# VectorE takes half of the picks of three items, gathered by pick column, into x_out

## The reference, cut to what matters

```
t = rms_norm(x, g_ffn)
q = t @ w_q                                  # 8 heads, two halves of 64
s = q . sub_keys; top 16 of each half; sums of pairs; top 16 of 256 -> ids, gates = softmax
act = gelu(einsum('td,thkd->thk', t, expert_u[ids]))
x  += einsum('thk,thkd->td', gates * act, expert_v[ids])
```

## Time and profile before

| | |
|---|---|
| median of 3 runs | 3340.63 us |
| profiled execution, its span | 3345.7 us, 23941 instructions |
| PE, PEld | 2192.0 us (66%), 765.3 us (23%) |
| DVE | 2166.7 us (65%) |
| ACT | 306.1 us (9%) |
| POOL | 2069.9 us (62%) |
| DMA | 1201.37 MB, mean 359 GB/s |

### The profile page before, as it was taken

The page is one execution under the profiler, slowest core; times in us unless marked ns, Lnnn a source line. Parts: engine busy times, 40 slices in busy tenths (PEclk is TensorE's granted clock), DMA queues, the critical chain, the costliest instruction groups (busy, mean ns, idle before and its releaser), DMA issues.

```text
span 3345.7 us, 23941 instructions
## 1 busy us (share of the span) xinstructions
PE 2192.0 (66%) x7260; PEld 765.3 (23%) x7260; DVE 2166.7 (65%) x5654; ACT 306.1 (9%) x657; POOL 2069.9 (62%) x2196
## 2 busy tenths in 40 slices
PE   8366776557644774688955376657895627564498
PEld 6112322112212121123312122212331212110122
DVE  4868488758777767635387967864618797636500
ACT  3100111101000001010101000000010010000000
POOL 1565665666666665566665656666666665666665
PEclk9698888778877987789977687878997868776699
DMA  6799998999999999999998999999999999999998
GB/s 248 286 365 332 368 363 329 378 379 343 373 368 339 367 374 409 410 400 365 364 362 324 385 337 359 368 365 383 360 356 343 349 365 332 384 373 377 380 375 326
DMA packets 331693, 1201.37 MB, mean 359 GB/s; under 512 B 40999, under 2 KB 41385, under 8 KB 329516
## 3 DMA queue, kind: packets, MB, share of 16 engines
q0 software_dynamic: 313344, 1140.99, 89.8%
q1 hardware_dynamic: 16988, 49.42, 3.9%
q10 hardware_dynamic: 1232, 9.44, 0.7%
HBM read 1188.82 MB, written 10.87 MB: 359 GB/s over the span
## 4 chain that ended last, share of the span: by engine, by line
DVE 26%; POOL 25%; issue 15%; another core or an unknown queue 15%; PE 13%; DMA 5%; ACT 1%; DVEq 0%; ACTq 0%; POOLq 0%
POOL rows L691 25%; DVE rows L1732 11%; PE acc L1208 7%; DVE psB L1405 4%; DMA rows<-in_expert_v,idsT 2%; DMA rows<-in_expert_u,ids 2%; PE psB L1143 1%; DVE work L1493 1%; DVE work L1486 1%; DVE work L1483 1%; PE psA L1056 1%; DVE work L1527 1%; DVE work L1533 1%; DVE work L1539 1%
## 5 line engine op out<-in xcount | busy, mean ns | idle before, releaser
L1208 PE MATMUL acc<-rows,strip 128*32 128x512 f32 x4352 | 1394.8, 658 | 462.9 <-DMA rows<-in_expert_v,idsT 305.0
L1732 DVE CUSTOM_DVE_ANT_0 rows<-rows,psH 128x1024 f32<-128x1024 f32 x1088 | 1288.3, 1218 | 336.2 <-DMA rows<-in_expert_u,ids 227.6
L691 POOL DMA_INDIRECT rows<-in_expert_v,idsT x1088 | 1030.6, 947 | 619.6 <-issue 273.0
L691 POOL DMA_INDIRECT rows<-in_expert_u,ids x1088 | 1024.1, 941 | 604.0 <-issue 326.0
L1208 PEld LDWEIGHTS acc<-rows,strip 128*32 128x32 f32 x4352 | 338.7, 116 | 1431.8 <-issue 955.0
L1405 DVE SCALAR_TENSOR_TENSOR psB<-zbuf,chan,psB 128x128 f32<-128x128 f32 (+1 forms) x827 | 202.8, 328 | 21.3 <-DVE psB L1405 16.6
L999 PE MATMUL psA<-w_out_sb,hT 128*128 128x512 f32 x288 | 153.8, 680 | 47.2 <-issue 35.1
L1039 PE MATMUL psB<-w_in_sb,hT 128*128 128x512 f32 x288 | 143.8, 649 | 56.9 <-DVE hT L1386 31.1
L1143 PE MATMUL psB<-w_q_sb,hT 128*128 128x512 f32 x288 | 142.0, 643 | 57.9 <-issue 37.5
L1739 DVE TENSOR_TENSOR x_out<-acc,x_out 128x1024 f32<-128x1024 f32 x10 | 12.2, 1222 | 248.9 <-PE acc L1208 176.6
L1056 PE MATMUL psA<-w_in_sb,hT 128*128 128x512 f32 x288 | 141.5, 646 | 1.7 <-DVEq L1573 1.7
(11 more groups left out here) (227 smaller groups left out, 1403.9 us busy)
## 6 DMA issues: line engine op xcount, KB each, us to landing
rows<-in_expert_u,ids POOLq DMA_INDIRECT x1088
rows<-in_expert_v,idsT POOLq DMA_INDIRECT x1088
w_in_sb<-in_w_in SPq DMA_DIRECT2D x4, 2176.0 KB, 30.7
w_out_sb<-in_w_out SPq DMA_DIRECT2D x2, 4096.0 KB, 18.6
w_q_sb<-in_w_q SPq DMA_DIRECT2D x2, 4096.0 KB
x_out<-x_mid SPq DMA_DIRECT2D x10, 512.0 KB
w_in_sb<-in_w_in ACTq DMA_DIRECT2D x2, 2176.0 KB, 22.8
x_mid<-x_mix SPq DMA_DIRECT2D x8, 512.0 KB
```

The source lines that it names most:

```text
L691: nc.gpsimd.indirect_dma_start(out=rows[:, j, :], out_offset=None, in_=table[:, :], in_offset=bass.IndirectOffsetOnAxis(ap=index, axis=0))\
L1208: last = nc.tensor.matmul(acc[LS * a:LS * (a + 1), half:half + 512], strip[:, first:first + LS], rows[:, at % RING, half:half + 512], star ...
L1732: nc.vector.tensor_tensor_reduce(rows[:, j, :], rows[:, j, :], psH[:, :], 1.0, 0.0, ALU.mult, ALU.add, dots[:, r:r + 1]).then_inc(s_free[j ...
```

## The change

The 128 picks of items 3, 6 and 9 are parted (SHARED = {3: 2, 6: 2, 9: 2}). Picks 0 to 63 are summed by TensorE as before, but in the quartered order, with 64 v gathers in place of 128. Picks 64 to 127 become a third kind of gather, "w": partition t gets the expert_v row of token t's r-th pick (index ids[:, r]), and VectorE adds coef[:, r] times this row to x_out. The w gathers of items 3 and 6 stand in ticks 12 to 26 of loops 4 and 7, where there is no v gather left; those of item 9 stand between its last 16 v gathers in loop 10. The number of gathers, 2176, and their bytes stay.

```diff
+SHARED = {3: 2, 6: 2, 9: 2}
...
+V_SHARED = [2] * 8 + [6, 7, 7, 6] + [0] * 15 + [2.5] * 8 + [2, 0, 4, 4, 2, 2, 2]
+W_WEIGHT = [0] * 12 + [2] + [4] * 12 + [7, 7] + [0] * 15
...
-V_OWN = {..., 4: V_ALONE, ..., 7: V_ALONE, 8: V_SHORT}
+V_OWN = {..., 4: V_SHARED, ..., 7: V_SHARED, 8: V_SHORT}
...
-          3: ..., 4: [(0, 36, 3, 0, 128), (37, 42, 4, 0, 14)],
+          3: ..., 4: [(0, 36, 3, 0, 64), (37, 42, 4, 0, 14)],
...
-          6: ..., 7: [(0, 36, 6, 0, 128), (37, 42, 7, 0, 14)],
+          6: ..., 7: [(0, 36, 6, 0, 64), (37, 42, 7, 0, 14)],
...
-          10: [(0, 42, 9, 48, 128)]}
+          10: [(0, 42, 9, 48, 64)]}
+
+W_PLAN = {4: (12, 27, 3, W_WEIGHT), 7: (12, 27, 6, W_WEIGHT), 10: (0, 42, 9, [1] * 42)}
...
-          ("both", 9, (10, 20), (11, 0))]
+          ("both", 9, (10, 0), (11, 0))]
...
+    def by_fours(v):
+        return v < QUARTERED or v in SHARED
+
+    def sums(v):
+        return SPICK * SHARED[v] if v in SHARED else width(v)
...
+    def w_at(n, tick):
+        if n not in W_PLAN:
+            return []
+        t0, t1, v, weight = W_PLAN[n]
+        return [("w", v, r) for r in share(weight, t0, t1, sums(v), picks(v), tick)]
...
+                elif kind == "w":
+                    table, index = ev, ids[:, i:i + 1]
...
+            def clear(v, g, k):
+                if g < 2 and v and by_fours(v) != by_fours(v - 1):
+                    for q in range(0, 1) if by_fours(v) else range(1, COPIES):
+                        step(nc.scalar.copy(laid_off(q)[:, k % 2 * GROUP:(k % 2 + 1) * GROUP], strip[:, 0:GROUP]))
+                    settle()
...
-                    if m < QUARTERED:
+                    if by_fours(m):
                         for part in range(QUARTERS):
                             last = turn_quarter(psA[:, LS * part:LS * (part + 1)], idf[m], part)
...
-                turn_tile(n, psH, coef).then_inc(s_cturn, 1)
+                if n in SHARED:
+                    for part in range(QUARTERS):
+                        last = turn_quarter(psH[:, LS * part:LS * (part + 1)], coef, part)
+                else:
+                    last = turn_tile(n, psH, coef)
+                last.then_inc(s_cturn, 1)
...
+            def add_picks(v, r):
+                j = AT["w", v, r] % RING
+                if r == sums(v):
+                    dve.wait_ge(s_coef, weighed(v))
+                    dve.wait_ge(s_xo, moved(1 + next(i for i, (what, u, _, _) in enumerate(X_PLAN) if u == v and what != "norm")))
+                else:
+                    done(dve, ("w", v, r - 1))
+                landed(dve, ("w", v, r))
+                nc.vector.scalar_tensor_tensor(out=x_out[:, :], in0=rows[:, j, :], scalar=coef[:, r:r + 1],
+                                               in1=x_out[:, :], op0=ALU.mult, op1=ALU.add).then_inc(s_free[j], 1)
...
             def take_sums(i, v):
                 n = spread(v)
                 done(dve, last_v(v))
+                if v in SHARED:
+                    done(dve, ("w", v, picks(v) - 1))
...
-                    picked = u_at(n, tick)
+                    picked = u_at(n, tick) + w_at(n, tick)
```

More of the change, by code:

```diff
@@ L53 @@
 V_LIGHT = [1] * 8 + [4] * 4 + [0.5] * 13 + V_LATE
[L54 removed]
+V_OWN = {0: V_QUARTERS[0], 1: V_QUARTERS[1], 2: V_CONV, 3: V_LIGHT, 4: V_SHARED, 5: V_SHORT, 6: V_LIGHT, 7: V_SHARED, 8: V_SHORT}
 U_END = [27, 27, 26, 26, 8, 26, 26, 8, 26, 26]
@@ L184, in build @@
     FETCHES = opening() + [key for n in range(ITEMS + 1) for tick in range(0 if n else 6, TICKS)
-                           for key in v_at(n, tick) + u_at(n, tick)]
+                           for key in v_at(n, tick) + u_at(n, tick) + w_at(n, tick)]
     AT = {key: i for i, key in enumerate(FETCHES)}
@@ L198, in last_v @@
     def last_v(v):
-        return "v", v, width(v) - 1
+        return "v", v, sums(v) - 1
     def place(v, i):
-        return i % 4, i % LS // 4 if v < QUARTERED else i // 4
+        return i % 4, i % LS // 4 if by_fours(v) else i // 4
     def index_column(v, i):
         a, b = place(v, i)
-        return SPICK * (i // LS) + 8 * a + b if v < QUARTERED else per_band(v) * a + b
+        return SPICK * (i // LS) + 8 * a + b if by_fours(v) else per_band(v) * a + b
     def per_band(v):
@@ L216, in spread @@
         return P if is_sample(v) else width(v)
-    GROUPS = [(v, g) for v in range(ITEMS) for g in range(width(v) // GROUP)]
+    GROUPS = [(v, g) for v in range(ITEMS) for g in range(sums(v) // GROUP)]
     def groups_at(n, tick):
@@ L836, in lay_out_quarter @@
                     done(act, ("v", u, GROUP * (ahead + 1) - 1))
+                clear(v, g, k)
                 for q in range(COPIES):
@@ L839, in lay_out_quarter @@
                     dst = laid_off(q)[r, k % 2 * GROUP:(k % 2 + 1) * GROUP].rearrange("p (b a) -> p b a", a=4)
-                    src = coefT[r, v, LS * part:LS * (part + 1)].rearrange("p (a b) -> p b a", a=4)
+                    src = coefT[r, v % 2, LS * part:LS * (part + 1)].rearrange("p (a b) -> p b a", a=4)
                     step(nc.scalar.copy(dst, src[:, 2 * g4:2 * g4 + 2, :]))
@@ L850, in lay_out @@
                     done(act, ("v", u, GROUP * (before + 1) - 1))
-                if v == QUARTERED and g < 2:
-                    for q in range(1, COPIES):
-                        step(nc.scalar.copy(laid_off(q)[:, k % 2 * GROUP:(k % 2 + 1) * GROUP], strip[:, 0:GROUP]))
-                    settle()
+                clear(v, g, k)
                 dst, src = laid[:, k % 2 * GROUP:(k % 2 + 1) * GROUP], coefT[:, v % 2, 0:width(v)]
@@ L934, in _ @@
                     for v, g in groups_at(n, tick):
-                        if v < QUARTERED:
+                        if by_fours(v):
                             lay_out_quarter(v, g)
@@ L1204, in add_tokens @@
                     a, b = place(v, i)
-                    first = (k % 2 * GROUP + i % GROUP + 1) * LS - 1 - (QUARTERS * b if v < QUARTERED else b)
-                    start, stop = i < 4, i + 4 >= width(v)
+                    first = (k % 2 * GROUP + i % GROUP + 1) * LS - 1 - (QUARTERS * b if by_fours(v) else b)
+                    start, stop = i < 4, i + 4 >= sums(v)
                     for half in (0, 512):
@@ L1733, in take_row, with take @@
                                                ALU.mult, ALU.add, dots[:, r:r + 1]).then_inc(s_free[j], 1)
+            def add_picks(v, r):
[8 more added lines that the diff above has]
+                                               in1=x_out[:, :], op0=ALU.mult, op1=ALU.add).then_inc(s_free[j], 1)
+            def take(key):
+                kind, m, r = key
+                if kind == "u":
+                    take_row(m, r)
+                else:
+                    add_picks(m, r)
             def take_sums(i, v):
@@ L1783, in _ @@
                                 if picked:
-                                    take_row(n, picked.pop(0)[2])
+                                    take(picked.pop(0))
                             weigh(n, part)
@@ L1792, in _ @@
                             if picked:
-                                take_row(n, picked.pop(0)[2])
-                    for _, _, r in picked:
-                        take_row(n, r)
+                                take(picked.pop(0))
+                    for key in picked:
+                        take(key)
 _INS = ['x_prompt', 'x_sample', 'state_pool', 'state_dwconv', 'state_shortconv', 'g_mix', 'w_in', 'w_pool',
```

## The result

The kernel after takes 3375.57 us (median of 4 runs, 3369.77 to 3385.29) against 3339.24 us for the kernel before on the same chip. The ratio is 1.0125 with a 95% interval of 1.0107 to 1.0142, or 36 us slower by the medians. Forecast was no change. The profiled execution has a span of 3383.4 us, 37.7 more than the span of before.

The account below looks back on a forecast made before the run. The prediction took the kernel as bound by its stream of 2176 gathers, held in places by engine chains. Terms +1.0 - 0.2 - 2.0 - 0.6 + 2.7 = +0.9 us on 3340.6 gave 3341.5 us, range 3320 to 3366.

Parts of the forecast that it names:

- Ticks 0 to 11: First part of loops 4 and 7, paced by the DMA: 74 gathers instead of 81, 110.1 us and 106.5 us.
- The w step: VectorE's addition in ticks 12 to 26: 1.28 us each, 1.32 apart in step with GpSimd, no cost from the shared port.
- TensorE is no hindrance: Ticks 12 to 26: norms, query and scores fit between w steps (45.0 us busy of 110.9); the 28.97 us wait goes.
- From the first w gather to the routing: Loops 4 and 7: 5.8 us landing, 84.5 w steps, 4.7 other VectorE work, 2 waits make 97.0; 97.4 us taken.
- Routing with what follows: Last part of loops 4 and 7, from the routing's start to the gather it releases: 65.6 and 68.8 us.
- about 74 us: Beside loop 4's routing: the time in which the DMA has 62 us of work, from 43 gathers.
- 12 for the one at the end: GpSimd's wait for TensorE near the end of loops 4 and 7 grows from 5 to about 12 us.
- Loop 10: Last 80 gathers, 64 moved to VectorE: 1.41 us each for 1.44, -2.0 us; landing to sum -0.6 more.
- The 410 GB/s of the trace: Stream rate seen late in loop 9, 1.28 us a gather; it kept a faster pace possible.
- The turns: 16 small matmuls turning expert numbers between routing and the next item's sums, 0.9 us three times: +2.7 us.
- the slow one: Rival: w steps in ticks 12 to 26 over 1.32 us apart, from port-delayed gathers or mixer waits; 3368.5 us, chance 0.22.
- point of decision: The slow rival decides from about 1.32 us a w step on, where loop 4's sum breaks even.

Follow-up runs that it names:

- after_again: The kernel after, unchanged, run again on one of the slower chips: ratio 1.0128 to the kernel before.
- half_steps: The kernel after with w steps on columns 0 to 511 only, upper half of the w picks' sum left out: 1.0113 to the kernel before.
- tensor_kept_going: The kernel after with 90 added TensorE matmuls that change no sum in ticks 12 to 26 of loops 4 and 7: 1.0196 to the kernel before.
- order_of_item_9: The kernel before with only item 9 in quartered order, all 128 picks by TensorE, no w gathers, on the faster chip: 1.0001 to the kernel before.

## Why the prediction was wrong, step by step

- Ticks 0 to 11: 110.1 forecast, 110.5 measured in loop 4; 106.5 and 110.2 in loop 7. Right, with loop 7 3.7 too low.
- The w step: 1.32 us in step with GpSimd, no port cost. Right: 15.81 us for 12, the w gather's mean 1058 ns. The Trainium skill, GPSIMD Engine Reference, section 1 (Specifications), has GpSimd contend with VectorE instructions that have two SBUF inputs. The trace agrees with the rule by that 1058 against the 939 ns of a u gather, but in the sum it costs nothing here.
- "TensorE is no hindrance": **the step that failed.** The forecast took 45.0 us of recorded work in a 110.9 us window of u gathers as proof that norms, query and scores fit between w steps, and counted 2 us for waits. They were 16.5 and 18.8 us (18.3 and 17.7 ahead of the scores alone in after_again), and 113.3 + 116.3 - 2 x 97.4 = 34.8 us is nearly all of the loss. The recorded busy time hid it: the query that begins in that window, at 1901.5, had its copy 34.5 us after its first matmul, outside the window, though its last record ended after 16.4. I had not set the copy beside the records. In the trace of before, the query of loop 5 and the copy that waits for it:

```profile
1901.47 16.38 PE L1143 MATMUL psB<-w_q_sb,hT 128*128 128x512 f32 x32 [13.74 <-DVE hT L1386]
...
1935.99 1.07 ACT L792 COPY x_mix<-psB 128x512 f32<-128x512 f32 x2 [1.13 <-remote]
```

- From the first w gather to the routing, on VectorE alone: 97.4 forecast. Right where VectorE did not wait in between: 97.6 in loop 7, 97.7 and 98.0 in after_again. On the faster chip its steps take the same 91.4 us, but the first of them starts 12.4 us after its gather was issued, where the sum had 5.8 and the kernel after 5.1 and 6.1, and the routing comes at +103.8.
- Routing with what follows: 65.6 and 68.8 forecast, 66.1 and 65.9 measured. Right in loop 4, 2.9 too high in loop 7, and right that the gathers missing beside it are lost: the DMA at 0.71 and 0.68. (The "about 74 us" beside this sum fits no part of it.) GpSimd's waits for TensorE grew in this window from 8.7 to 24.4 us in loop 4 and from 13.6 to 36.2 in loop 7, where I had written 12 for the one at the end. Only that last one stayed 5 us (4.98 and 4.92); ahead of it GpSimd now waits 19.46 and 16.28 us. TensorE in turn waited 27.80 and 25.15 us with item 4's and item 7's sums for VectorE's addition of the item before (line 1789), which stands in the routing. In loop 4:

```profile
1714.44 0.94 POOL L712 DMA_INDIRECT rows<-in_expert_v,idsT  x1 [19.46 <-PE acc L1238]
```

```profile
1710.54 5.97 PE L1238 MATMUL acc<-rows,strip 128*32 128x512 f32 x32 [27.80 <-DVE x_out L1789]
```

- Loop 10: 2.0 less forecast, 0.3 measured (113.1 against 113.4). From the last gather's issue to the sum 7.1 us against 7.7: the 0.6 forecast. The 410 GB/s of the trace did not come here (363).
- The turns: +2.7 forecast. The order by itself measured 1.0001 and 1.0003, with intervals about 3 and 4.5 us wide to either side, so 2.7 us can't be told from nothing.
- The rivals: the time, 3375.6, lies beyond the slow one (3368.5), in its place and by its chain (routing late, few gathers beside it). Its cause was half named: "mixer steps wait for TensorE at the lower clock with w rows behind them". Its other half, w steps slower than 1.32 us, is refuted by the rows, and half_steps shows that the steps' length did not matter. Its point of decision was wrong too, since the w steps kept to 1.32. That the time lies beyond its 3368.5, then, does not bear out its mechanism.

## What to carry to other kernels

Before moving work off an engine, look at that engine in a stage of the same kernel where it already has nothing beside its chain, and measure from the first instruction to the consumer that waits for its semaphore, not to the last record. Where a serial stage of fixed length (here 66 us of routing) follows, each transfer taken from beside it is lost, and one taken from a stage paced by transfers and put there is won: 12 gathers a loop were 21 us. In this kernel 64 w steps between the steps of the norms delayed the chain behind them, and 32 of them, with 13 v gathers left to TensorE, cost nothing that could be told.

## What the runs showed of the hardware

On the slower chips 16 matmuls of 128x512 in float32 took 16 to 59 us to their semaphore when TensorE had no other work, and 16 to 27 with v sums between in loops 4 and 7. The granted clock alone does not explain it: at 1.2 GHz throughout, half the rate of tensor_kept_going's 0.89 us a matmul at a granted clock of 1.00 (35.9 us for 40.5 matmuls), they would take 28 us by estimate. On one chip the same query took 15 to 17 us every time, and the last 80 gathers ran at GpSimd's 1.25 us each (98.5 us for 79 spacings in order_of_item_9) where the others had 1.44. With 64 full w steps and no more than two added matmuls a tick, VectorE's waits of about 15 to 19 us a loop moved between layer norm, transposes and query as steps were moved, and did not leave. What makes TensorE late on those chips, and whether the transfers have a part in it, the runs do not settle.
